# Taps of the prompt's convolution spread through four tiles of the retention output stage, with its mean two tiles and its variance one tile later

## The reference, cut to what matters

```python
h = rms_norm(x, g_mix_pre)
q, k, v, g_ret, ca, cb, ga, gb = jnp.split(h @ w_in, offs, axis=-1)
o, r_new = retention_chunkwise(rope(q), rope(k) * DK ** -0.5, v, r0)   # 4 heads
y_ret = (jax.nn.silu(g_ret) * layer_norm(o, ret_gn_gain)) @ w_ret_out
u = ca * jax.nn.sigmoid(cb)
padded = jnp.concatenate([c0, u], axis=1)
z = depthwise_conv(padded, conv_w) + conv_b                # 31 taps per channel
z = jax.nn.silu(layer_norm(z, conv_ln_g, conv_ln_b))
y_conv = z @ w_conv_out
merged = jax.nn.sigmoid(ga + b_ga) * y_ret + jax.nn.sigmoid(gb + b_gb) * y_conv
x = x + rms_norm(merged @ w_o, g_mix_post)
# then the feed-forward part: (silu(h2 @ w_gate) * (h2 @ w_up)) @ w_down
```

## Time and profile before

| | us |
|---|---|
| median of 3 runs | 1511.04 |
| the profiled execution | 1508.52 |
| its span | 1506.8 |
| PE busy | 1459.2 (97%) |
| DVE busy | 1141.5 (76%) |
| ACT busy | 678.7 (45%) |
| POOL busy | 271.4 (18%) |

### The profile page before, as it was taken

One profiled execution on the slowest core, in us unless ns is written; L12 is line 12 of the kernel. 1 busy time (PEld: TensorE's weight loads), 2 busy tenths in 40 slices (PEclk: granted clock), 3 DMA queues, 4 the chain that ended last, 5 costly groups with the idle time before them and its releaser, 6 DMA issues.

```text
span 1506.8 us, 25271 instructions
## 1 busy us (share of the span) xinstructions
PE 1459.2 (97%) x9684; PEld 1370.5 (91%) x9684; DVE 1141.5 (76%) x1771; ACT 678.7 (45%) x996; POOL 271.4 (18%) x254
## 2 busy tenths in 40 slices
PE   9999999999999999999998999999999999999997
PEld 8998878788999999999988988788799999999996
DVE  6999898999757666885478988898995766666544
ACT  5344434446455444443353445445554645434432
POOL 4991111120200001556100001112111000000000
PEclk9999999999999999999999999999999999999998
DMA  8447664846544344445444566758654442544453
GB/s 331 143 154 258 240 238 182 321 164 214 158 160 164 116 154 144 149 153 159 163 145 157 202 212 235 275 195 300 219 185 143 142 151 84 169 153 152 154 156 121
DMA packets 64971, 275.48 MB, mean 183 GB/s; under 512 B 7280, under 2 KB 7536, under 8 KB 55664
## 3 DMA queue, kind: packets, MB, share of 16 engines
q1 hardware_dynamic: 53280, 193.49, 38.1%
q0 software_dynamic: 11600, 80.74, 15.1%
HBM read 230.30 MB, written 43.89 MB: 182 GB/s over the span
## 4 chain that ended last, share of the span: by engine, by line
PE 76%; DVE 17%; ACT 3%; issue 2%; DMA 1%; POOL 0%; DVEq 0%; ACTq 0%
PE bank L467 22%; PE bank L469 22%; PE bank L468 22%; DVE wlo L1180 5%; DVE acc L1223 3%; DVE state L1254 3%; PE bank L676 2%; PE bank L637 1%; PE bank L618 1%; DVE go L1330 1%; PE bank L492 1%; DVE x L1577 1%; PE bank L586 1%; DVE tmp L1575 1%; PE bank L488 1%
## 5 line engine op out<-in xcount | busy, mean ns | idle before, releaser
L467 PE MATMUL bank<-hhi,whi 128*128 128x320 f32 x1976 | 636.1, 322 | 10.8 <-DVE hlo L1180 5.0
L1180 DVE TENSOR_TENSOR wlo<-wring,whi 128x1024 fp32r<-128x1024 f32 x363 | 488.7, 1350 | 183.5 <-ACT whi L894 156.0
L469 PE MATMUL bank<-hhi,wlo 128*128 128x320 f32 x1976 | 611.5, 309 | 0.0
L468 PE MATMUL bank<-hlo,whi 128*128 128x320 f32 x1976 | 611.1, 309 | 0.0
L467 PEld LDWEIGHTS bank<-hhi,whi 128*128 128x128 f32 x1976 | 372.0, 188 | 29.1 <-issue 22.7
L468 PEld LDWEIGHTS bank<-hlo,whi 128*128 128x128 f32 x1976 | 372.2, 188 | 8.8 <-issue 7.7
L469 PEld LDWEIGHTS bank<-hhi,wlo 128*128 128x128 f32 x1976 | 371.7, 188 | 0.0
L894 ACT ACTIVATE whi<-wring 128x1024 fp32r<-128x1024 f32 x264 | 276.9, 1054 | 206.0 <-PE bank L469 205.2
L1223 DVE SCALAR_TENSOR_TENSOR acc<-up,par,acc 128x256 f32<-128x256 f32 x480 | 219.6, 524 | 0.3
L920 ACT ACTIVATE whi<-wring 128x1024 fp32r<-128x1024 f32 x96 | 101.2, 1054 | 60.8 <-PE bank L469 58.1
L467 PE MATMUL bank<-fhi,whi 128*128 128x320 f32 x352 | 110.7, 314 | 0.0
(11 more groups left out here) (193 smaller groups left out, 1898.2 us busy)
## 6 DMA issues: line engine op xcount, KB each, us to landing
wring<-w SPq DMA_DIRECT2D x364, 512.0 KB, 3.8
state<-r_in POOLq DMA_DIRECT2D x32, 1024.0 KB, 7.7
rs_out<-state POOLq DMA_DIRECT2D x32, 1024.0 KB, 5.1
rp_out<-pst POOLq DMA_DIRECT2D x8, 512.0 KB, 9.4
us<-c_in POOLq DMA_DIRECT2D x2, 1216.0 KB, 5.5
cs_out<-us POOLq DMA_DIRECT2D x2, 1216.0 KB, 8.7
cp_out<-up POOLq DMA_DIRECT2D x2, 1144.0 KB, 4.9
con<-consts POOLq DMA_DIRECT2D x1, 1421.0 KB, 9.5
```

Source lines behind the costliest of these rows:

```text
L467: pe.matmul(bank[g][:, 0:T], whi[j][:, k, :], hi, start=start and k == 0, stop=False)
L468: pe.matmul(bank[g][:, 0:T], whi[j][:, k, :], lo, start=False, stop=False)
L469: mm = pe.matmul(bank[g][:, 0:T], wlo[j][:, k, :], hi, start=False, stop=stop and k == n - 1)
L1180: return dve.tensor_tensor(dst, value, hi.bitcast(F32), ALU.subtract)
```

## The change

Taps are taken out of units 5, 7 and 8 of heads 1 to 3 (in the second layer out of 5 and 8), and in the second layer out of five units of the gate stage, and put into the retention output stage, which now has 21 taps in each layer: two in nearly every unit of its first four tiles. Since the last taps come later, the mean's matmul and copy go from tile 2 to tile 4, the subtractions from behind the product of tile 2 to ahead of the product of tile 4, the squares from tile 3 to tile 4, and the matmul of the variance from the end of tile 4 to the end of tile 5. ACT's logarithm stays in tile 5, behind its splits. No instruction is added or dropped: in the first layer 12 taps change place, in the second 15.

```diff
-HEAD_TAPS = ((6, 0, 3, 0, 2, 3, 0, 2, 2, 1, 3, 3), (7, 0, 3, 0, 2, 3, 0, 3, 2, 1, 3, 3), (5, 0, 3, 0, 0, 2, 0, 1, 1, 2, 3, 3))
-GB_TAPS = ((6, 0, 3, 4, 3, 1, 4, 0), (5, 0, 3, 3, 2, 1, 3, 0))
-RET_TAPS = ((2, 2, 2, 2, 1, 0), (1, 2, 2, 1, 0, 0))
+HEAD_TAPS = ((6, 0, 3, 0, 2, 1, 0, 1, 1, 1, 3, 3), (7, 0, 3, 0, 2, 1, 0, 2, 1, 1, 3, 3), (5, 0, 3, 0, 0, 0, 0, 1, 0, 2, 3, 3))
+GB_TAPS = ((6, 0, 3, 4, 3, 1, 4, 0), (4, 0, 3, 2, 0, 0, 2, 0))
+RET_TAPS = ((1, 2, 2, 2, 2, 2, 2, 2, 2, 2, 2, 0), (1, 2, 2, 2, 2, 2, 2, 2, 2, 2, 2, 0))
...
-                    if n == 2:
+                    if n == 4:
 
                         pe.wait_ge(conv_sum, l * 7 + 4)
                         pe.matmul(X[:, 0:T], ones_d[:, :], pairs[:, 0, :], start=True, stop=True).then_inc(stat_done, 1)
...
-                    if n == 4:
-                        pe.wait_ge(stat_read, l * STATS + (ST_CMEAN + 1))
-                        pe.wait_ge(conv_sum, l * 7 + 7)
-                        pe.matmul(X[:, 0:T], ones_d[:, :], sqz[:, 0, :], start=True, stop=True).then_inc(stat_done, 1)
+                        if n == 5 and p == 1:
+                            pe.wait_ge(stat_read, l * STATS + (ST_CMEAN + 1))
+                            pe.wait_ge(conv_sum, l * 7 + 7)
+                            pe.matmul(X[:, 0:T], ones_d[:, :], sqz[:, 0, :], start=True, stop=True).then_inc(stat_done, 1)
...
-                    if n == 2:
+                    if n == 4:
                         act.wait_ge(stat_done, l * STATS + (ST_CMEAN + 1))
                         act.activation(cmean[:, :], X[:, 0:T], ACT.Copy).then_inc(stat_read, 1)
-                    if n == 3:
...
-                        if n < 2:
+                        if n < 4:
                             conv_taps(l, RET_TAPS[l][3 * n + p])
 
+                    if n == 4:
+                        dve.wait_ge(stat_read, l * STATS + (ST_CMEAN + 1))
+                        for k in range(KT):
+                            dve.tensor_tensor(acc[:, k, :], acc[:, k, :], cmean[:, :], ALU.subtract).then_inc(conv_norm, 1)
```

More of the change, by code:

```diff
@@ L1517, in _ @@
                     dve.tensor_tensor(acc2[:, n, :], bank[(2 * n + 1) % 4][:, 0:T], sig[:, n % 4, :], ALU.mult).then_inc(ret_gated, 1)
[L1518 to L1521, removed]
                     if n >= 6:
```

## The result

| us | before | after |
|---|---|---|
| median, runs of the same chip | 1511.08 (4 runs, 1509.97 to 1511.49) | 1497.53 (4 runs, 1497.34 to 1497.99) |
| the profiled execution | 1508.52 | 1497.34 |
| its span | 1506.8 | 1495.5 |
| DVE busy | 1141.5 (76%) | 1144.1 (76%) |

After takes 0.9912 of the time before, interval 0.9895 to 0.9929: 13.5 us less, where 10.1 were forecast. The spans of the two traces differ by 11.3. The profiled execution of before is not one of its four runs, and at 1508.52 it was shorter than all of them.

The account below looks back on a forecast made before the run. DVE's taps ahead of the state updates and gated outputs were taken to make PE stop in the heads. Gains 7.1 + 2.2 + 0.2 + 0.6 = 10.1 us off the median of 1511.04 gave 1500.9 us, range 1498 to 1505.

Parts of the forecast that it names:

- First layer's heads: Heads 1 to 3: gated outputs come 2.37 us earlier per head, all gained by PE; 7.1 us, bounds 4.2 and 8.7.
- Rival 1: Heads: ACT paces the chain behind unit 7, only the updates' stall goes; gain 4.2 + 0.6, 1506.2 us; chance 0.13.
- Second layer's heads: Heads 1 to 3: PE's waits at L667 and L573, together 0.73 us a head, go; 2.2 us, bounds 0 and 2.2.
- L805: Retention stage, first layer: the mean's matmul no longer waits for POOL's pair sums; gains 0.6 us, bounds 0 and 0.8.
- The variance's margin: Retention stage: POOL's sums of squares end half a microsecond before PE asks; cost 0, up to 1 us per layer.
- rival 2: Retention stage: the variance's sums are late, PE stands 1.5 us a layer before L817; gain 7, 1504 us; chance 0.07.
- Gate stage: Second layer: six taps go, but most turns into waiting for PE; gain 0.2 us, bounds 0 and 1.6.
- The retention stage takes the taps free: Retention stage: two taps per unit cost nothing, as DVE needs 2.86 of 3.52 us per unit.
- rival 4: Retention stage: taps cost 0.79 us an instruction, as beside POOL, so the kernel is slower, 1515.7 us; chance 0.03.
- Rival 3: Heads: stalls return at the next place, on state loads or key transposes; no change, 1510 us; chance 0.05.
- Taking the trace's gain off the median: Whole kernel: median of before, 1511.04, is 2.5 above the profiled execution; the 10.1 us gain comes off it, giving 1500.9.
- The range: Whole kernel: 1498 to 1505 us; the forecast's own bounds 1498.5 to 1503, extended for median scatter and over the 1504 case.

Follow-up runs that it names:

- e4: After's code, but against the tables of before only the two taps of unit 5 in heads 1 to 3 moved, both layers: 1501.59 us, ratio 0.9942.
- e14: e12 again, unchanged, on the same chip as e13: 1502.16 us, ratio 0.9946.
- e3: After with the second layer's tap tables of before: 1501.16 us, ratio 0.9942.
- e12: After with one tap put back in unit 7 of heads 2 and 3, first layer (two fewer in its retention stage): 1501.79 us, ratio 0.9944.
- e13: e12 with PE's stops before L573 in heads 2 and 3 filled by 8 unread matmuls each: 1500.66 us, ratio 0.9937.
- e5: Before with PE's first-layer stops ahead of L573 filled by unread matmuls, 6 (head 1) or 10 (heads 2 and 3): 1511.33 us, ratio 1.0006.
- e11: e5 with 4 and 8 filling matmuls in place of 6 and 10: 1509.82 us, ratio 0.9995 against before.
- e9: After, unchanged, a second trace and more executions: 1498.39 us, ratio 0.9921 against before.
- e10: Before, unchanged, a third trace and more executions: 1510.1 us, ratio 1.0.
- e2: After's code with the tables of before, so only the tail's new order: 1510.55 us, ratio 0.9998 against before.

## Why the mechanism held and the gain was forecast 3.4 us short

- **First layer's heads, 7.1 forecast, 7.1 measured** (2.37, 2.39, 2.38 a head). Both halves are shown apart: e4 takes the 1.58 of unit 5 without touching L573's 1.9, and head 3 of e14 puts back 0.78 with the tap of unit 7 alone. Rival 1, that ACT paces the chain, is refuted by the same pair. What is left of L573 is 1.14 where the working gave 0.9: unit 7 also became 0.2 shorter, so PE came that much earlier to the same `go`.
- **Second layer's heads, 2.2 forecast, 3.3 measured.** This step failed. The term, and its upper bound of 2.2 with it, was the sum of idle times that the records show, 0.37 and 0.36 a head. By the starts of units the stops are 0.58 and 0.52. The prediction had noted that a gap under 0.15 doesn't appear, had used starts in the first layer, and read idle times here. DVE had enough to give: by the prediction's own working, with 0.58 for 0.37, it could come 0.58 + 0.69 = 1.27 earlier, and the stops to fill were 1.1.
- **L805, 0.6 forecast, 0.83 measured**, for the same reason (0.55 shown); it is just above its bound of 0.8. The variance's margin was 0.4 where 0.5 was worked out, so rival 2 stayed away by four tenths. **Gate stage, 0.2 forecast, 0.24 measured** in the second layer (unit 71, 6.64 to 6.40; in e4, which leaves the gate stage's taps, it is 6.64).
- **The retention stage takes the taps free**: PE has no wait there in either layer of after that before hadn't, and rival 4 is refuted by the 1.67 row. Rival 3, that the stops come back later, is refuted by every head of after and e3.
- **Taking the trace's gain off the median of three runs.** This step failed too. Of the 3.4 us missed, 1.2 are the sizes above (11.3 - 10.1), and 2.2 are between the traces' difference and the medians'. The prediction took the median for a constant 2.5 above the trace. But the first trace of before was a short execution, without the slow stretch in head 3: the later two have it and end at 1508.3, 1.5 above. Of the 64 executions of before on the four later chips none was as short as 1508.52, and their median is 1510.13. A stretch at the lower clock behind L573 goes with the stop that the change shortens, by the 6 of 14 against 0 of 18 heads. How much of the median it is stays open: six stretches of 1.55 in 14 heads are 0.66 a head or 1.3 for two (an estimate), e12 puts it at 3.4 - 1.6 = 1.8, e13 against e14 at 1.5, e5 and e11 at nothing. Nor is the clock of after the higher one over whole executions: the granted clocks listed for them average 0.9945 in after's four and 0.9936 in e9, and 0.9941 to 0.9949 in before by chip.
- The four executions of after were also at the good end: in e9 it took 1498.39. Typical against typical is 1510.1 to 1498.4, 11.7 us, and the spans of the traces of e10 and e9, 1508.3 and 1496.6, differ by the same 11.7. So the first medians lay 0.9 above what is typical of before and 0.9 below what is typical of after: 1.8 of the 2.2 is the choice of executions and no gain of the change. How much of the 11.7 is the lower clock in before these runs can't tell.
- **The range.** The upper bounds of the prediction's own terms add up to 8.7 + 2.2 + 1.6 + 0.8 = 13.3, which off 1511.04 is 1497.7; the 1498.5 given as the forecast's own bound, and the 1498 of the range, don't follow from them.

## What to carry to other kernels

Measure a stop by the distance between starts of equal stretches of work, against a stretch that has none. The idle time in a record of pipelined work is a lower bound, and it was 0.15 to 0.3 us short each time here, 1.1 us over the six stops of the second layer's heads. Where a chain ends in a stop, take work away from ahead of its end, in each of its links (unit 5, then unit 7), and leave alone what stands behind it (unit 8). After a contention is removed, ask which engine had been hidden by it: of 1.66 us saved on DVE, PE got 0.43, because ACT was next. Look at two or three traces of the kernel before, not one, when the change is worth less than 1%: here they differed by one 1.5 us step.

## What the runs showed of the hardware that was not expected

- PE's clock can be at its lower level for a part of a unit after a stop of only 1.9 us, in an engine whose records show no other idle time in the 5 us before it: granted clock 0.77 in one unit, 5.72 to 7.26 us. It isn't certain: the same stop with the same work around it had none in 8 of 14 cases. After stops of 1.15 or less it was not seen there (18 heads). The gate stages fit this: the second layer's stop at L667 is 0.9 to 1.7 in all 16 traces and none has the lower level there, while the first layer's is 2.0 to 2.9 in 14 of them and nine have it. Of the two long stops for the load of a state, the 2.2 of e13 has it and the 2.1 of e5 hasn't. Unit 8 of the second layer (stage CIN) takes 0.2 to 1.2 us more than in the first trace of before in ten traces, and in all of these but after's the stretch at the lower level there is longer too.
- In the gate stage of the first layer a stop of PE and the clock trade against each other. The window of 355 to 363 us of before, and then of e2, where the clock stayed up:

```profile
355.00:363.00 8.00, 5.25 (x30) 4.93 (x29) 7.48 (x15) 5.70 (x8) 1.07 (x1) 0.79 0.73 261
```

```profile
355.00:363.00 8.00, 5.57 (x42) 5.31 (x41) 7.48 (x15) 6.13 (x9) 1.08 (x1) 1.00 0.70 264
```

PE did 42 matmuls there in place of 30, unit 71 fell from 9.21 to 7.46, and unit 72 rose from 3.52 to 4.89, because PE came earlier to a wait that DVE ends (e2):

```profile
367.53 0.39 PE L467 MATMUL bank<-ghi,whi 128*128 128x320 f32 x1 [1.21 <-DVE glo L1179]
```

With 0.3 more in units 68 and 69 nothing is left: the lower clock cost this stage no time.

- POOL's addition (128x640) made DVE's half longer by 1.66 us, though it took only 1.59 itself. By these two numbers DVE got next to nothing done in that half while POOL ran.
